# Latent attention queries made token-major by fours of heads and turned by TensorE, with changes of order in the gates and at the start

## The chip, the cores and the metric

The kernel is one program on one core of a Trainium2 chip. The metric is the device time of one execution in microseconds (us), as the median of repeated runs. Profiles are of one further execution of the same program.

## What is computed

Two transformer blocks are applied to one sequence of 256 tokens, 1024 channels wide, all in 32-bit floats. The part that the change rewrites is the second attention of the second block: its queries come from a latent of 768 channels, 96 channels a head, are normalised over these 96, and the last 32 of them are rotated by position.

```python
qb = jnp.einsum('bsr,re->bse', rms_norm_2(c_q, cq_norm_g), w_uq)
qb = qb.reshape(b, s, N_HEADS_B, QK_HEAD_DIM_B)          # 8 heads x (64 + 32)
...
qb = rms_norm_2(qb, qnorm_b_g)
kb = rms_norm_2(kb, knorm_b_g)
qb = jnp.concatenate([qb[..., :QK_NOPE_DIM],
                      apply_rope(qb[..., QK_NOPE_DIM:], positions)], axis=-1)
kb = jnp.concatenate([kb[..., :QK_NOPE_DIM],
                      apply_rope(kb[..., QK_NOPE_DIM:], positions)], axis=-1)
out_b = causal_block_attention(qb, kb, vb).reshape(b, s, WIDTH_B)
```

apply_rope multiplies the 32 channels by cosines and adds the same channels, their halves swapped, times signed sines. Before all this stands a first block (a gated linear recurrence, a spatial gate, three gate projections, a wide feed-forward layer), and in the second block another attention (heads of 64 channels) shares the stretch with the latent one.

## The kernel before

**Weights.** All weights stream through four slots of `raw` (128 x 2048 floats, a "unit"), brought by DMAs of the SP queue as soon as unit u-4 has been used (`unit_used`). ScalarE (ACT in the profile) rounds a unit to `whi` (`split_hi`, called three units ahead as `ahead(u)`), VectorE (DVE) makes the remainder `wlo` (`split_lo`), and TensorE (PE) computes each product in three matmuls (`mm3`: whi with xh, whi with xl, wlo with xh).

**Order.** Every engine runs one program that is written out by hand, and waits on semaphores. Nothing is reordered at run time, so an instruction that waits holds up everything behind it on its engine.

**The attention stretch.** There are eight pairs of heads, p = 0 to 3 of the first attention and 4 to 7 of the latent one. For each pair, `qk(p)` makes logits on PE, `logits_row(p)` scales and biases them on DVE, `softmax_exp(p)` is on ACT, `normalise(p)` on DVE, `turn(p)` transposes the probabilities on PE, `probs_copy(p)` copies them on ACT, `pv(p)` multiplies them with the values on PE, and `heads_hi(p)`, `heads_lo(p)` split the result. Between these steps PE is given other work: the latent queries (`queries`, six calls of eight blocks, while pairs 0 to 3 pass), the keys' transposes (`keys_turned`), and the output projection (`wo_part`). A head's queries are channel-major: the weights stand still in PE, 256 tokens stream, and the rows 96 to 127 of a head hold a second copy of its last 32 channels, halves swapped (the weights hold these columns twice).

**Queries on other engines.** `queries_evac(j)` (ACT, four calls, one for two heads) copies the swapped rows, squares, and copies with the gain, and signals `uq_ev`. GpSimd (POOL) runs `rotate(j)`, three operations of 32 x 512, and signals `q_rot`. `queries_stats(j)` (PE) sums the squares over channels with 16 tiny matmuls, DVE adds epsilon (`queries_factor`), and POOL's `head_factors` takes the power -1/2. PE's `qk(p)` of a latent pair waits for `q_rot`.

**Gates and start.** In units U_GA to U_GB+3 ACT first rounds the next unit and then evacuates the finished gate with its sigmoid or silu. At the start PE runs 14 products of ones before the first real product, and the input's four parts and the first weights arrive in the order of `PIECES`.

Of the kernel before, what the change touches and what calls it, by code (L numbers as in the profile page):

```python
# [68 lines left out]
HEADS_BANK = (7,) * 7 + (4,)  # L69

# [100 lines left out]
PIECES = ((0, 1), (2,), (3, 4), (5, 6, 7, 8, 9))  # L171
# [27 lines left out]

def raw_count(u):  # L200

    return 16 * sum(2 if by_rows(v) else 1 for v in range(u % SLOTS, u + 1, SLOTS))
# [35 lines left out]
def build_blocks(nc, w, xT, pT, par, cst, lvl, sgw, sgb, lnr, rel, oneh, maskb, pos, out):  # L238
    scratch = nc.dram_tensor("bias_scratch", [HEADS, 512], F32, kind="Internal").ap()
    ctx = ExitStack()  # L240
    with ctx:
# [31 lines left out]
        gkb = sb("gkb", [P, 1])  # L273
        nti = sb("nti", [P, 32], I32)
# [15 lines left out]
        def keys_part(v):  # L290

            return v[:, U_UK % SLOTS, :].rearrange("p (n c) -> p n c", c=P)[:, :, 0:64]

# [73 lines left out]
        qb, kb, qsw, sqq = view(48, 8), view(56, 8), view(64, 8), view(72, 8)  # L367
# [8 lines left out]
        cosk, sink, cosq, sinq = (view(80 + i, 1) for i in range(4))  # L376
# [11 lines left out]
        def _(sp):  # L388
# [7 lines left out]
            for u in range(3, UNITS):  # L396
                if u >= SLOTS:
                    sp.wait_ge(sem("unit_used"), u + 1 - SLOTS)
                if by_rows(u):
                    for i in range(2):  # L400
                        dst = raw[:, u % SLOTS, 1024 * i:1024 * i + 1024].rearrange("p (n c) -> p n c", n=2)
                        src = w[stored(u - u % 2 + i)].rearrange("p (n c) -> p n c", n=2)[:, :, columns(u % 2)]
                        sp.dma_start(dst, src).then_inc(sem(f"raw_in{u % SLOTS}"), 16)
                else:
                    sp.dma_start(raw[:, u % SLOTS, :], w[stored(u)]).then_inc(sem(f"raw_in{u % SLOTS}"), 16)
# [8 lines left out]
        def _(pool):  # L414
            pool.dma_start(cst_s[:, :], cst).then_inc(sem("cst_in"), 16)
            nc.gpsimd.memset(half_s[:, :], -0.5).then_inc(sem("half"), 1)
            pool.wait_ge(sem("half"), 1)
            pool.wait_ge(sem("raw_in3"), 16)
# [68 lines left out]
            pool.dma_start(ang[64:96, 0, :].bitcast(I32), pos[0:1, :].broadcast_to([32, T])).then_inc(sem("pos_in"), 16)  # L487
# [11 lines left out]
            def rotate(j):  # L499

                pool.wait_ge(sem("uq_ev"), j + 1)
                q_, w_ = qb[64:96, 2 * j:2 * j + 2, :], qsw[64:96, 2 * j:2 * j + 2, :]
                nc.gpsimd.tensor_tensor(q_, q_, cosq[64:96, 0:1, :].broadcast_to([32, 2, T]), ALU.mult).then_inc(sem("rot"), 1)
                nc.gpsimd.tensor_tensor(w_, w_, sinq[64:96, 0:1, :].broadcast_to([32, 2, T]), ALU.mult).then_inc(sem("rot"), 1)
                pool.wait_ge(sem("rot"), 2 * j + 2)
                nc.gpsimd.tensor_tensor(q_, q_, w_, ALU.add).then_inc(sem("q_rot"), 1)
                pool.wait_ge(sem("q_rot"), j + 1)

            head_factors("sk", 32, 16)
            pool.wait_ge(sem("rope"), 1)  # L510
            for j in range(4):
                rotate(j)
                head_factors("sq", 48 + 4 * j, 4, j + 1)
            for s in ("bias_in", "pos_in", "maskb_in"):
# [5 lines left out]
        def _(act):  # L520
            A = nc.scalar.activation

            def split_hi(u):
# [3 lines left out]
                hi, full = (keys_part(v) if u == U_UK else v[:, slot, :] for v in (whi, raw))  # L527
# [123 lines left out]
            for u in range(4, 32):  # L651
# [6 lines left out]
                if u == U_WB - 1:  # L658
                    heads_hi_turned(0)
                    heads_hi_turned(1)  # L660
                if not U_ZI <= u < U_GA:
# [27 lines left out]
                elif u % 2 == 1:  # L689
                    dst, func, m = ((ga, ACT.Sigmoid, u - U_GA) if u < U_ZG else  # L690
                                    (zg, ACT.Silu, u - U_ZG) if u < U_GB else (gb, ACT.Sigmoid, u - U_GB))
                    filled(u)
                    for s in range(2):
                        evac(u - 1 + s, dst[:, s, columns(m // 2)], func, scale=rtok[:, 0, s:s + 1])
# [216 lines left out]
            def rope_copy():  # L911
# [3 lines left out]
                for t in range(2):  # L915
                    A(krt_sq[:, t, :], src[:, t, 0:32], ACT.Square, accum_out=rs[:, 16 + t:17 + t])
                A(krt, src[:, :, 32:64], ACT.Copy).then_inc(sem("krt"), 1)
# [6 lines left out]
            def queries_evac(j):  # L924
                if j < 3:
                    act.wait_ge(sem("uq_mm"), j + 1)
                else:
                    filled(U_UQ + 2)
                b = j % 3
                src = ps[b][0:96, :].rearrange("p (h t) -> p h t", h=2)  # L930
                hs = slice(2 * j, 2 * j + 2)
                A(qsw[64:96, hs, :], ps[b][96:128, :].rearrange("p (h t) -> p h t", h=2), ACT.Copy)
                A(sqq[0:96, hs, :], src, ACT.Square)
                A(qb[0:96, hs, :], src, ACT.Copy, scale=col("qb", 0, 0, 96)).then_inc(sem("uq_ev"), 1)
# [14 lines left out]
            heads_hi(0)  # L949
            queries_evac(0)  # L950

# [4 lines left out]
            queries_evac(1)  # L956
            queries_evac(2)

            probs_copy(2)
            softmax_exp(3)  # L960
            heads_hi(2)
# [4 lines left out]
            queries_evac(3)  # L966

            for i in range(4, 6):
                probs_copy(i - 1)
                softmax_exp(i)  # L970
                heads_hi(i - 1)
                if i == 4:
                    keys_evac(2)
                    keys_evac(3)
                normalise_second(i)
# [53 lines left out]
        def _(dve):  # L1029
# [12 lines left out]
            def split_lo(u):  # L1042

                slot = u % SLOTS
                dve.wait_ge(sem("hi_ready"), u + 1)
                lo, full, hi = (keys_part(v) if u == U_UK else v[:, slot, :] for v in (wlo, raw, whi))
# [461 lines left out]
            def logits_row(p):  # L1508
# [3 lines left out]
                if p >= 4:  # L1512
                    dve.wait_ge(sem("sq_fac"), p - 3)
                for hh in range(2):
# [3 lines left out]
                    r0, r1 = (h, 16 + h) if p < 4 else (48 + 4 * (p - 4) + hh, 48 + 4 * (p - 4) + 2 + hh)  # L1518
# [1239 lines left out]
```

## Time and profile before

| what | value |
|---|---|
| median of 3 runs | 817.52 us (816.78 to 817.81) |
| the profiled execution | 817.01 us, of which the span from first to last instruction is 814.8 us |
| PE busy | 807.4 us, 99% of the span |
| DVE, ACT, POOL busy | 578.2, 466.0, 116.0 us (71%, 57%, 14%) |
| TensorE's granted clock | 1.000 of full speed |
| DMA | 143.85 MB, mean 177 GB/s |

Busy time of PE counts overlapping matmuls once, so 99% says that PE is hardly ever without a matmul, not that it is at its peak. The distance from the start of one group of matmuls to the start of the next is what a group costs.

### The profile page before, as it was taken

How to read it: one execution, taken by the hardware profiler on the slowest of the kernel's cores; microseconds unless marked ns; L12 is line 12 of the kernel's file. 1: busy time of each engine (PE TensorE's matmuls, PEld its weight loads, DVE VectorE, ACT ScalarE, POOL GpSimd, SP SyncE). 2: the span in 40 equal slices, each digit the busy share in tenths (PEclk: the TensorE clock that was granted, in tenths of full speed). 3: DMA queues.
4: the chain of work that ended last, by engine and by line, in shares of the span. 5: the costliest groups of instructions: out<-in, count | busy, mean ns of one | idle time of the engine just before them, and what ended most of it. 6: DMA issues, size and time to landing. Idle time of an engine off the chain costs nothing.

```text
span 814.8 us, 14269 instructions
## 1 busy us (share of the span) xinstructions
PE 807.4 (99%) x6160; PEld 715.4 (88%) x6160; DVE 578.2 (71%) x717; ACT 466.0 (57%) x602; POOL 116.0 (14%) x78
## 2 busy tenths in 40 slices
PE   9999999999999999999999999999999999999998
PEld 8999988788788998888888799998899888888886
DVE  6868995896666677666666687698967866556653
ACT  7679774563634674445544565456887644544442
POOL 0102780672000000000000000000482000000000
PEclk9999999999999999999999999999999999999999
DMA  9844444444553655555556555555332655555641
GB/s 316 294 157 162 159 169 133 156 158 155 168 205 108 234 181 187 180 201 197 172 200 202 171 198 186 182 173 191 105 104 74 218 180 202 197 173 198 207 156 51
DMA packets 30222, 143.85 MB, mean 177 GB/s; under 512 B 2978, under 2 KB 5042, under 8 KB 15824
## 3 DMA queue, kind: packets, MB, share of 16 engines
q1 hardware_dynamic: 28976, 139.47, 50.0%
q0 software_dynamic: 1040, 3.43, 1.2%
q8 instruction: 48, 0.79, 0.4%
q14 instruction: 14, 0.11, 0.0%
q10 hardware_dynamic: 144, 0.04, 0.0%
HBM read 141.87 MB, written 1.06 MB: 175 GB/s over the span
## 4 chain that ended last, share of the span: by engine, by line
PE 95%; DVE 2%; ACT 1%; DMA 1%; issue 1%; POOL 0%; SPq 0%
PE ps L1829 8%; PE ps L1830 8%; PE ps L1831 8%; PE ps L2235 7%; PE ps L2228 7%; PE ps L2140 6%; PE ps L2142 6%; PE ps L2141 6%; PE ps L1897 5%; PE ps L1900 4%; PE ps L1903 4%; PE ps L2233 4%; PE ps L2230 4%; PE ps L2006 1%; DMA raw<-w 1%; PE ps L1855 1%
## 5 line engine op out<-in xcount | busy, mean ns | idle before, releaser
L1047 DVE TENSOR_TENSOR wlo<-raw,whi 128x2048 fp32r<-128x2048 f32 x128 | 292.8, 2289 | 85.9 <-ACT whi L528 84.6
L528 ACT ACTIVATE whi<-raw 128x2048 fp32r<-128x2048 f32 x128 | 243.8, 1906 | 140.4 <-DMA raw<-w 140.4
L1829 PE MATMUL ps<-xx,whi 128*128 128x256 f32 x552 | 159.2, 288 | 0.0
L1830 PE MATMUL ps<-xx,whi 128*128 128x256 f32 x552 | 156.1, 283 | 0.0
L1831 PE MATMUL ps<-xx,wlo 128*128 128x256 f32 x552 | 156.1, 283 | 0.0
L1829 PEld LDWEIGHTS ps<-xx,whi 128*128 128x128 f32 x552 | 105.7, 191 | 1.5 <-issue 0.7
L1830 PEld LDWEIGHTS ps<-xx,whi 128*128 128x128 f32 x552 | 105.8, 192 | 0.1
L1831 PEld LDWEIGHTS ps<-xx,wlo 128*128 128x128 f32 x552 | 105.7, 192 | 0.0
L2140 PE MATMUL ps<-whi,xx 128*128 128x512 f32 x216 | 84.1, 390 | 0.0
L2141 PE MATMUL ps<-whi,xx 128*128 128x512 f32 x216 | 84.1, 389 | 0.0
L2142 PE MATMUL ps<-wlo,xx 128*128 128x512 f32 x216 | 84.0, 389 | 0.0
L1897 PE MATMUL ps<-whi,xx 128*128 128x512 f32 x176 | 70.5, 401 | 0.7 <-ACT work L540 0.7
L1399 DVE TENSOR_TENSOR work<-ps,work 128x256 f32<-128x256 f32 x64 | 26.8, 420 | 62.6 <-ACT work L763 62.6
L447 POOL TENSOR_TENSOR work<-work 128x512 f32<-128x512 f32 x28 | 58.7, 2117 | 84.3 <-DVE work L1191 45.3
L1900 PE MATMUL ps<-whi,xx 128*128 128x512 f32 x176 | 68.7, 390 | 0.0
L1903 PE MATMUL ps<-wlo,xx 128*128 128x512 f32 x176 | 68.6, 390 | 0.0
L2235 PE MATMUL ps<-xx,whi 128*128 128x512 f32 x256 | 64.1, 392 | 0.0
L2228 PE MATMUL ps<-xx,whi 128*128 128x512 f32 x256 | 63.3, 389 | 0.0
L2228 PEld LDWEIGHTS ps<-xx,whi 128*128 128x128 f32 x256 | 47.9, 188 | 10.0
L2235 PEld LDWEIGHTS ps<-xx,whi 128*128 128x128 f32 x256 | 46.0, 189 | 8.2
L767 ACT ACTIVATE xx<-work 128x512 fp32r<-128x512 f32 x27 | 17.1, 633 | 57.3 <-DVE work L1421 26.9
L2142 PEld LDWEIGHTS ps<-wlo,xx 128*128 128x128 f32 x216 | 40.5, 188 | 8.4
(298 smaller groups left out, 1272.7 us busy)
## 6 DMA issues: line engine op xcount, KB each, us to landing
raw<-w SPq DMA_DIRECT2D x112, 1024.0 KB, 4.9
raw<-w SPq DMA_DIRECT2D x34, 512.0 KB, 5.0
raw<-w SPq DMA_DIRECT2D x8, 256.0 KB, 6.6
x<-xT SPq DMA_DIRECT2D x4, 256.0 KB, 5.5
work<-bias_scratch POOLq DMA_DIRECT2D x1, 1024.0 KB, 8.2
out<-x SPq DMA_DIRECT2D x3, 256.0 KB, 2.5
work<-lnr POOLq DMA_DIRECT2D x1, 512.0 KB, 6.5
work<-sgw POOLq DMA_DIRECT2D x1, 512.0 KB, 7.2
```

The source lines that it names most:

```text
L528: A(hi, full, ACT.Copy).then_inc(sem("hi_ready"), 1)
L1047: V.tensor_tensor(lo, full, hi.bitcast(F32), ALU.subtract)\
L1829: mm(out, hi, xh[:, tile, :], start=start, stop=False, skip_group_check=skip)
L1830: mm(out, hi, xl[:, tile, :], start=False, stop=False, skip_group_check=skip)
L1831: return mm(out, wlo[:, slot, at:at + width], xh[:, tile, :], start=False, stop=stop, skip_group_check=skip)
L1897: mm(o, xh[:, t, xs], wh, start=first, stop=False)
L1900: mm(o, xl[:, t, xs], wh, start=False, stop=False)
L2140: mm(o, xh[:, base + kk, xs], whi[:, slot, wc], start=first, stop=False, skip_group_check=True)
L2141: mm(o, xl[:, base + kk, xs], whi[:, slot, wc], start=False, stop=False, skip_group_check=True)
L2142: return mm(o, xh[:, base + kk, xs], wlo[:, slot, wc], start=False, stop=end, skip_group_check=True)
L2228: mm(o[:, :], whi[:, u % SLOTS, w(k)], xx[:, base + k, :, :], start=k == 0, stop=False)
L2235: last = mm(o[:, :], whi[:, u % SLOTS, w(k)], xx[:, base + k, :, :], start=False, stop=k == 7, skip_group_check=True)
```

## The change

The queries of four heads are now made token-major: 128 tokens stand still in PE and 384 columns of weights (four heads of 96) stream, so that tokens lie on partitions. The doubled weight columns are not loaded: units U_UQ, U_UQ+1 and U_UQ+2 are gathered by 5, 9 and 4 DMAs with rows of 96 columns, and hold 5, 5 and 2 steps of 384 columns. `queries_evac(g)` (two calls) takes two PSUM banks each with a square and a copy of 128 x 384; DVE sums the squares along the free axis; POOL rotates on 128 partitions, four operations for four heads and 128 tokens; PE then transposes the result (`queries_turned(j)`, four transposes, four calls) and ACT copies it with the gain (also named `queries_turned(j)`, signal `q_n`). The cosine and sine table is transposed too, and copied by ACT (`qrope`) before `krt` is signalled.

```diff
 (PE)
-            for n in range(14):
+            for n in range(11):
...
-            def queries_stats(j):
-                pe.wait_ge(sem("uq_ev"), j + 1)
-                pe.wait_ge(sem("head_ml"), j + 2)
-                for s in range(2):
-                    for hh in range(2):
-                        last = head_stats(272 + 4 * j + 2 * s + hh, sqq, 2 * j + hh, s)
...
+                    for t in range(2):
+                        if k == 0 and (g, t) != (0, 0):
+                            if (g, t) == (1, 1):
+                                pe.wait_ge(sem("uq_ev"), 1)
+                            else:
+                                pe.wait_ge(sem("uk_ev"), g + 1)
+                        o = ps[QUERY_BANKS[g][t]][:, 0:384]
+                        xs, wc = slice(t * P, (t + 1) * P), slice(384 * at, 384 * at + 384)
+                        mm(o, xh[:, k, xs], whi[:, u % SLOTS, wc], start=k == 0, stop=False)
+                        mm(o, xl[:, k, xs], whi[:, u % SLOTS, wc], start=False, stop=False)
+                        last = mm(o, xh[:, k, xs], wlo[:, u % SLOTS, wc], start=False, stop=k == 5)
...
+            def queries_turned(j):
+
+                pe.wait_ge(sem("q_rot"), 2 * (j // 2) + 2)
+                if j % 2:
+                    pe.wait_ge(sem("q_n"), j)
+                for hh in range(2):
+                    for t in range(2):
+                        last = nc.tensor.transpose(ps[TURN_BANKS[j]][0:96, hh * T + t * P:hh * T + (t + 1) * P],
+                                                   qtok[:, t, 2 * j + hh, :], ident)
+                last.then_inc(sem("qt_mm"), 1)
...
-            queries(32, 40)
+            queries(4)
+            queries_turned(0)
             qk(3)
             turn(2)
-            queries_stats(0)
-            queries(40, 48)
+            queries(5)
+            queries_turned(1)
             pv(2)
             keys_turned(0)
+            pe.wait_ge(sem("q_n"), 2)
             pe.wait_ge(sem("uq_ev"), 3)
             wo_part(0, 0, range(4), (1, 2))
...
 (POOL)
-            pool.dma_start(cst_s[:, :], cst).then_inc(sem("cst_in"), 16)
...
+            pool.wait_ge(sem("x_in3"), 16)
+            pool.dma_start(cst_s[:, :], cst).then_inc(sem("cst_in"), 16)
 (ACT)
+                if u in (U_GA, U_ZG, U_GB):
+                    A(warm[:, :], half_s[:, 0:1], ACT.Silu if u == U_ZG else ACT.Sigmoid)
+                if u >= U_GA and u % 2 == 1:
+                    dst, func, m = ((ga, ACT.Sigmoid, u - U_GA) if u < U_ZG else
...
+                    filled(u)
+                    for s in range(2):
+                        evac(u - 1 + s, dst[:, s, columns(m // 2)], func, scale=rtok[:, 0, s:s + 1])
                 if not U_ZI <= u < U_GA:
                     ahead(u)
 (DVE)
-                factor_input("sq", ps[7][:, a:a + 4], 48 + 4 * j, 4, 96)
+                link(V.reduce_sum(sums, qsq[g].rearrange("p s (h c) -> p (s h) c", c=96), AX))
+                V.tensor_scalar(sums, sums, 96 * EPS, None, ALU.add).then_inc(sem("sq_eps"), 1)
```

PE around the fifth pair, in the kernel before: the tail of `turn(3)` (L2410), then the 16 small sums of `queries_stats(1)` (L1923), the output products (L1829 to L1831, twelve in all, three shown), `pv(3)` (L2431 to L2435), `keys_turned(1)` (L2463) and the next output product.

```order
L2410 MATMUL ps<-cst_s,work 128x128 x5
L1923 MATMUL ps<-cst_s,work 32x1 [waits head_ml,uq_ev]
L1923 MATMUL ps<-cst_s,work 32x1 x15
L1829 MATMUL ps<-xx,whi 128x256 [waits head_ml]
L1830 MATMUL ps<-xx,whi 128x256
L1831 MATMUL ps<-xx,wlo 128x256
...
L2435 MATMUL ps<-work 64x128 x2
L2463 MATMUL ps<-cst_s,work 96x128 [waits head_l,k_n]
L2463 MATMUL ps<-cst_s,work 96x128 x7
L1829 MATMUL ps<-xx,whi 128x256 [waits head_ml,lo_ready,uq_ev]
```

The same place in the changed kernel (the lines' numbers have moved):

```order
L2478 MATMUL ps<-cst_s,work 128x128 x5
L2572 MATMUL ps<-cst_s,work 96x128 [waits q_rot]
L2572 MATMUL ps<-cst_s,work 96x128 x3
L1897 MATMUL ps<-xx,whi 128x256 [waits head_ml]
L1898 MATMUL ps<-xx,whi 128x256
L1899 MATMUL ps<-xx,wlo 128x256
...
L2500 MATMUL ps<-work 64x128 x2
L2572 MATMUL ps<-cst_s,work 96x128 [waits q_n,q_rot]
L2572 MATMUL ps<-cst_s,work 96x128 x3
L2518 MATMUL ps<-cst_s,work 96x128 [waits head_l,k_n]
L2518 MATMUL ps<-cst_s,work 96x128 x7
L1897 MATMUL ps<-xx,whi 128x256 [waits head_ml,lo_ready,q_n]
```

The 16 sums are gone, two groups of four transposes (L2572) have come in, and the second group and the output product behind the keys' transposes now wait for `q_n`, a copy on ACT.

ACT at the fifth pair in the changed kernel: `softmax_exp(4)` (L939), `queries_turned(2)` (L999), `heads_hi(3)` (L958), `keys_evac(2)` and `keys_evac(3)` (L983), `queries_turned(3)` (L999), `normalise_second(4)` (L947).

```order
L939 ACTIVATE work<-work 128x128 [waits head_l]
L939 ACTIVATE work<-work 128x256
L939 ACTIVATE work<-work 128x128
L939 ACTIVATE work<-work 128x256
L999 ACTIVATE work<-ps0,gqb 96x512 [waits qt_mm]
L958 ACTIVATE xx<-ps7 128x256 [waits head_pv]
L983 ACTIVATE work<-ps4,gkb 96x512 [waits kt_mm]
L983 ACTIVATE work<-ps3,gkb 96x512 [waits kt_mm]
L999 ACTIVATE work<-ps0,gqb 96x512 [waits qt_mm]
L947 ACTIVATE work<-work 128x128 [waits head_rec]
```

In the kernel before the two rows L999 are not there, and the same ten places hold only the exponentials, `heads_hi(3)`, the two `keys_evac` and `normalise_second(4)`.

POOL, the power for the keys (L547 of the changed kernel) and the rotation of the first four heads, as it is now:

```order
L547 TENSOR_TENSOR nt<-nt,half_s 128x16 [waits sk_eps]
L556 TENSOR_TENSOR work<-work 128x128 [waits uq_ev,krt,sk_fac]
L560 TENSOR_TENSOR work<-work 128x4x16 x2
L562 TENSOR_TENSOR work<-work 128x4x32 [waits rot]
L556 TENSOR_TENSOR work<-work 128x128 [waits uq_ev,q_rot]
L560 TENSOR_TENSOR work<-work 128x4x16 x2
L562 TENSOR_TENSOR work<-work 128x4x32 [waits rot]
L547 TENSOR_TENSOR nt<-nt,half_s 128x8 [waits sq_eps,q_rot]
```

Before, three operations of 32x512 stood here for two heads, and PE's first reader of them was `qk(4)`; now eight smaller ones stand for four heads, and PE's first reader is `queries_turned(0)`, ahead of `qk(3)`.

## Rows read from the trace of the kernel before

**Rows 1.** The page, first part: busy time, share, instructions.

```profile
PE 807.4 (99%) x6160; PEld 715.4 (88%) x6160; DVE 578.2 (71%) x717; ACT 466.0 (57%) x602; POOL 116.0 (14%) x78
```

**Rows 2.** Waits of PE: total us, times, longest us.

```profile
PE ps L1897 <- ACT work L540: 0.7, 1, 0.7
```

**Rows 3.** Timeline of PE: start, us, first block of queries, second pair.

```profile
565.16 0.38 PE L1829 MATMUL ps<-xx,whi 128*128 128x256 f32 x1
...
568.22 0.49 PE L2397 MATMUL ps<-work 64*128 64x128 f32 x4
...
569.08 0.88 PE L2410 MATMUL ps<-cst_s,work 128*128 128x128 f32 x6
```

**Rows 4.** Timeline of PE, from the fourth pair to the fifth.

```profile
585.03 0.49 PE L2397 MATMUL ps<-work 64*128 64x128 f32 x4
...
586.93 0.43 PE L1923 MATMUL ps<-cst_s,work 96*32 96x1 f32 x32
...
591.16 1.08 PE L2463 MATMUL ps<-cst_s,work 128*96 128x128 f32 x8
592.00 0.36 PE L1829 MATMUL ps<-xx,whi 128*128 128x256 f32 x1
...
594.95 0.61 PE L2397 MATMUL ps<-work 96*128 96x128 f32 x4
...
600.63 0.36 PE L1829 MATMUL ps<-xx,whi 128*128 128x256 f32 x1
```

**Rows 5.** Timeline of ACT: krt's copy, a pair's copies, exponentials, keys' copies.

```profile
568.63 0.24 ACT L917 ACTIVATE work<-ps 128x64 f32<-128x64 f32 x1
...
578.40 0.87 ACT L893 ACTIVATE work<-ps 128x384 f32<-128x384 f32 x2 [1.92 <-PE ps L2410]
...
588.79 0.40 ACT L879 ACTIVATE work<-work 128x128 f32<-128x128 f32 x1 [0.17 <-DVE work L1531]
...
590.47 0.19 ACT L879 ACTIVATION_READ_ACCUMULATOR work<-work 128x1 f32 x1
...
591.84 1.26 ACT L922 ACTIVATE work<-ps,gkb 96x512 f32<-96x512 f32 x2 [0.18 <-PE ps L2463]
```

**Rows 6.** Timeline of DVE: keys' scaling; end of the fifth pair's logits.

```profile
580.06 1.23 DVE L1689 TENSOR_TENSOR work<-work,nt 128x1024 f32<-128x1024 f32 x1
581.20 2.92 DVE L1692 TENSOR_TENSOR work<-work,nt 128x256 f32<-128x256 f32 x2
...
597.92 0.08 DVE L1523 DVE_READ_ACCUMULATOR2_ANT work<- 128x1 f32 x1
```

**Rows 7.** Timeline of POOL: powers (L495) and rotations (L503).

```profile
577.11 2.92 POOL L495 TENSOR_TENSOR nt<-nt,half_s 128x16 f32<-128x16 f32 x1 [54.02 <-DVE nt L1680]
580.11 2.30 POOL L503 TENSOR_TENSOR work<-work 32x512 f32<-32x512 f32 x1
...
605.43 1.01 POOL L495 TENSOR_TENSOR nt<-nt,half_s 128x4 f32<-128x4 f32 x1 [0.21 <-DVE nt L1504]
606.52 1.27 POOL L503 TENSOR_TENSOR work<-work 32x512 f32<-32x512 f32 x1
```

**Rows 8.** Timeline of PE, opening.

```profile
1.04 6.24 PE L1982 MATMUL ps<-work 128*128 128x128 f32 x28 [1.04 <-DVE work L1100]
7.04 0.71 PE L1950 MATMUL ps<-whi,xx 128*128 128x512 f32 x2
...
18.40 0.28 PE L1971 MATMUL ps<-xx,whi 128*128 128x256 f32 x1
```

**Rows 9.** Timeline of ACT, opening: the first weights' rounding.

```profile
5.91 0.63 ACT L569 ACTIVATE whi<-raw 128x512 fp32r<-128x512 f32 x1 [0.18 <-DMA raw<-w]
```

**Rows 10.** DMA issues: KB each, us to landing.

```profile
cst_s<-cst POOLq DMA_DIRECT2D x1, 99.0 KB, 5.1
```

**Rows 11.** Timeline of ACT at the gates.

```profile
206.33 1.28 ACT L540 ACT_TABLE_LOAD   x1
207.63 1.27 ACT L540 ACTIVATE work<-ps,rtok 128x512 f32<-128x512 f32 x2
```

More of the change, by code:

```diff
@@ L197, in by_rows, with query_place, query_runs, transfers @@
     return U_GA <= u < U_WB or U_WA <= u < U_WOUT
+QUERY_STEPS = (((0, 0), (0, 1), (0, 2), (0, 3), (0, 4)),
+               ((0, 5), (1, 0), (1, 1), (1, 2), (1, 3)),
+               ((1, 4), (1, 5)))
+def query_place(g, k):
+    n = next(n for n in range(3) if (g, k) in QUERY_STEPS[n])
+    return n, QUERY_STEPS[n].index((g, k))
+def query_runs(n):
+    runs = []
+    for h in range(HEADS):
+        ks = [k for g, k in QUERY_STEPS[n] if g == h // 4]
+        for u in range(3):
+            here = [k for k in ks if (6 * h + k) // 16 == u]
+            if here:
+                runs.append((h, here[0], len(here), u, (6 * h + here[0]) % 16))
+    return runs
+def transfers(u):
+    if U_UQ <= u < U_WO:
+        return len(query_runs(u - U_UQ))
+    return 2 if by_rows(u) else 1
 def raw_count(u):
-    return 16 * sum(2 if by_rows(v) else 1 for v in range(u % SLOTS, u + 1, SLOTS))
+    return 16 * sum(transfers(v) for v in range(u % SLOTS, u + 1, SLOTS))
 def z_index(u):
@@ L497, in head_factors, with rotate @@
                 pool.wait_ge(sem(name + "_fac"), turn)
[L499 to L507, printed above, removed]
[L509 to L514 removed]
+            def rotate(g, t):
+                n = 2 * g + t + 1
+                pool.wait_ge(sem("uq_ev"), n)
+                q_ = qtok[:, t, 4 * g:4 * g + 4, 64:96]
+                nc.gpsimd.tensor_tensor(turn_a, q_, qrope[:, t:t + 1, 0:32].broadcast_to([P, 4, 32]), ALU.mult).then_inc(sem("rot"), 1)
+                for half in range(2):
+                    other = qtok[:, t, 4 * g:4 * g + 4, 80 - 16 * half:96 - 16 * half]
+                    sines = qrope[:, t:t + 1, 32 + 16 * half:48 + 16 * half].broadcast_to([P, 4, 16])
+                    nc.gpsimd.tensor_tensor(turn_b[:, :, 16 * half:16 * half + 16], other, sines, ALU.mult).then_inc(sem("rot"), 1)
+                pool.wait_ge(sem("rot"), 3 * n)
+                nc.gpsimd.tensor_tensor(q_, turn_a, turn_b, ALU.add).then_inc(sem("q_rot"), 1)
+                pool.wait_ge(sem("q_rot"), n)
+            head_factors("sk", 32, 16)
+            pool.wait_ge(sem("krt"), 1)
+            for g in range(2):
+                rotate(g, 0)
+                rotate(g, 1)
+                head_factors("sq", 48 + 8 * g, 8, g + 1)
+            pool.wait_ge(sem("p_in"), 32)
+            for s in ("bias_in", "maskb_in"):
                 pool.wait_ge(sem(s), 16)
@@ L2481, in _, with queries @@
             rope_turned()
-            def queries(first, end):
-                for i in range(first, end):
-                    n, blk = divmod(i, 16)
-                    h, k = divmod(i, 6)
-                    j, u = h // 2, U_UQ + n
-                    if blk == 0:
+            def queries(i):
+                g, part = divmod(i, 3)
+                for k in (2 * part, 2 * part + 1):
+                    n, at = query_place(g, k)
+                    u = U_UQ + n
+                    if at == 0:
```

123 lines of the change are left out of this document (65 added, 58 removed).

## The prediction

> **What bounds the kernel now.** I read the page first, then the waits of PE, then the timelines of PE, ACT, DVE and POOL through the attention stretch, and last the opening and the gates. The page shows PE busy for 99% of the span [rows 1], and apart from the start its longest wait is 0.7 us, for a gate's evacuation [rows 2]. So time is what PE is given to do: a change gains what it takes off PE and loses every new wait of PE. Whether a wait is new is read from chains on ACT, DVE and POOL, whose shares look harmless as averages.
>
> **What PE is given less.** One block of query products, 24 matmuls of 256 columns, runs from 565.16 to the second pair's `qk` at 568.22, 3.06 us, or about 0.12 a matmul with 0.17 for entering [rows 3]. The new block has 12 matmuls of 384 columns. None of that width is in the trace. The 48 opening products of 512 columns take at most 11.36 us, 0.237 each [rows 8]; half-way between 0.12 and 0.237 is 0.178, and 12 of these with the entry are 2.3 us. Six blocks give -0.76 each, -4.6. The bounds are those of a matmul, 0.12 and 0.237: -8.7 to -0.3; half-way is near, since width is all that differs. The four groups of small sums take 0.43 each [rows 4]: -1.7. Sixteen transposes come in; eight of the keys' take 0.84 (591.16 to 592.00), 0.105 each [rows 4]: +1.7, and two for the position table +0.2. Net -4.4 us. If nothing waited, this would be the gain of the stretch.
>
> **What PE then waits for.** I walk it in the times of the trace, four places in order.
>
> First turn. PE would come to `turn(0)` at 565.16 + 0.2 + 2.3 + 0.86 (the step from 568.22 to 569.08 [rows 3]) = 568.5. It waits for `krt`, which ACT signals after the copy at 568.63 [rows 5], and the copy of the table now goes ahead of it with 0.2 to 0.25. So 569.1: PE waits 0.6, and is where it was before.
>
> First turning of queries. PE comes there after four more blocks, four times 0.76 earlier than before, at about 582.0. It waits for both rotations of the first four heads, which stand on POOL behind the power for the keys, 2.92 us for 16 elements [rows 7]. That power started at 577.11. It comes about 1.7 earlier: `qk(1)` is 0.56 earlier, and DVE's remainder of the last query unit shrinks by 1280 columns, 1.5 us at 1.23 per 1024 [rows 6], less 0.4 in which DVE then waits for ACT's exponentials. So it ends at 578.3. A rotation is four POOL operations, on 128, 64, 64 and 128 elements. 512 elements take 1.27 when nothing disturbs [rows 7]. Scaled by elements that gives 0.32 and 0.16; with the fixed part of the powers (16 elements 2.92, 4 elements 1.01, so 0.16 an element and 0.37 fixed) it gives 0.6 and 0.5. I take 0.45 and 0.3: two rotations 3.2 us with signals (2.0 to 4.5).
>
> POOL does not have this time to itself. The rotation at 580.11 took 2.30 against 1.27 of the same operation at 606.52 [rows 7], and it ended 1.1 us after DVE's scaling of the keys at 580.06 (1.23) had; the two following scalings of 256 elements took 2.92 together where 1.23 per 1024 gives 0.7 [rows 6]. These two engines take turns. Beside the new rotations stand the same three scalings (1.9) and the third pair's four normalisations (about 1.0), 2.9 in all; I take 2.3, since some fall where POOL waits for its own signals. Rotations end at 578.3 + 3.2 + 2.3 = 583.8. PE waits 1.8 us (0 if nothing is held, 3.7 by the upper bounds). The Trainium skill, in SBUF — State Buffer, section Who interferes with whom, says that a DVE instruction with two inputs in SBUF and a GpSimd instruction that reads it exclude each other for their whole length. By that rule all 2.9 are held and PE waits 2.4; the rows 6 and 7 agree with it, 2.30 against 1.27. With 0.45 for the transposes `qk(3)` is at 584.25 instead of 585.03: 0.8 early.
>
> Output products behind the keys' transposes. They use banks that ACT must have emptied of turned queries (`q_n` 2). From `qk(3)` to them it was 592.00 - 585.03 = 6.97 [rows 4]. Now the chain is: `qk` and DVE's logits to the start of the exponentials 3.4 (it was 588.79 - 585.03 = 3.76, with DVE late from its own work [rows 4, 5]), exponentials 1.8 (588.79 to 590.66 [rows 5]), four reads of 128 x 384 at 0.87 a pair, 1.6 [rows 5], a copy of 96 x 512, 0.6 (two take 1.26 [rows 5]), a signal 0.1: 7.5. So 0.5 is lost here, and 0.3 is left of the lead.
>
> Fifth pair. From `qk(4)` to the next output product it was 600.63 - 594.95 = 5.68 [rows 4], full of work. Now there are two hand-overs in a row. Logits end at 598.00, 3.05 after `qk(4)` [rows 4, 6], exponentials 1.8, the copy 0.6, signals 0.1: the fourth turning can start 5.55 after `qk(4)`. Then on PE its four transposes and four of the keys', 0.85, a latency of 0.25, on ACT two keys' copies 1.2 and the last queries' copy 0.6: 2.95 with signals. Together 8.5, 2.8 more than before. Behind the waiting matmul on PE stands the whole rest of the stretch, and its lead is gone: 2.5 late. The third and fourth groups of sums, 0.9, fall away after this place: +1.6 us at the end of the stretch. Sums and waits agree: -4.4 from work, +0.6, +1.8, and some 3.6 in the last two places.
>
> **The other parts.** Gates: the evacuation at 207.63 stood behind the rounding of the next unit and a table load of 1.28 [rows 11]; the gate's product is done before, and the load is now made early by a dummy. The 0.7 wait goes [rows 2]: -0.7 (0 to -0.8). Opening: three of 14 products of ones go, 6.0 / 14 each, so PE is free at 5.8 instead of 7.04 [rows 8], and its first weights are rounded at 5.91 + 0.63 = 6.5 [rows 9]: up to -0.5 there; of the 11.36 up to 18.40 [rows 8] some 0.4 are waits for parts in an order that now suits it better. Against this the constants leave 12 us later, took 5.1 us to land [rows 10], and PE wants them right after these products. I take -0.6 (0 to -1.0). The gathers of 96 columns have no row; ACT's idle time hides them, and late ones would delay the first exponentials.
>
> **Sum.** +1.6 - 0.7 - 0.6 = +0.3 on the profiled execution's 817.0, which is 0.5 below the median of the runs shown; against the median, 817.5 + 0.3 = 817.8 us. About 1.6 us either way, 0.2%, is what a measurement of this kernel can tell from no change.
>
> **Rivals.** (a) Rotations are short and not held, and ACT's copies fit beside other steps: the 1.8 go, and about half of the 2.8; the stretch ends at -1.5, the kernel at 814.8. For it: POOL is busy 14%. Against: the 2.30 against 1.27 of rows 7. (b) No new wait lasts: -4.4 - 0.7 - 0.6 = -5.7, 811.8 us. For it: 99% busy PE and all its work counted. Against: a chain from `qk(4)` that row by row is 8.5 us long. (c) Slower: POOL is the bound. With 0.6 and 0.5 an operation and 2.9 held, the first turning waits 3.7 instead of 1.8, and the second group, which starts only after its own power, comes late for the third turning by about 0.8; +0.3 + 2.7 = 820.5 us. It decides from about 0.55 an operation. (d) Slower: PE, idle for 2 us at a time where 0.7 was the longest, loses clock. The trace before grants full clock throughout. One block (2.3) and one pair's steps (1.5) at half speed would cost 3.8: 821.6 us. The skill's TensorE: Matmul & The Clock Gate, section What's actually happening, has the clock fall behind idle PE; no row here shows it.
>
> **How the numbers follow.** Forecast 0.40 (its own range 816.2 to 819.4), (a) 0.24, (b) 0.10, (c) 0.23, (d) 0.03. The range reaches past (a) and (c) and leaves out (b) and (d) and a little more: 813.6 to 820.8. Faster by over 0.2%: (a), (b) and 0.02 of the forecast, 0.36. Slower: (c), (d) and 0.04, 0.30. Within: 0.34.
>
> **What would show it.** Right: PE's waits list four new ones, for ACT's `krt` copy (0.6), for POOL's sum (about 1.8), and twice for ACT's copy of turned queries (about 1.5 each), and the gate's 0.7 is gone; DVE idles before the fourth pair's logits; a block of products takes 2.2 to 2.4. Wrong: POOL's operations well under 0.3 or over 0.55 us; a granted clock below 1; PE waiting for `cst_in` or for a gathered unit; and any chain of ACT that runs shorter than its rows say.

## The result and the profile after

The changed kernel takes 821.19 us (median of 10 runs, 819.7 to 825.12), the kernel before on the same chip 817.58 us (10 runs). The ratio is 1.004, with a 95% interval of 1.0024 to 1.0057: slower by 2.0 to 4.7 us. The forecast was 817.8 us with no measurable change, and the range ended at 820.8; both missed.

The profiled execution took 821.01 us with a span of 819.2, where that of before had 814.8. The page of the changed kernel, busy time, beside [rows 1]:

```profile
PE 803.3 (98%) x5972; PEld 708.3 (86%) x5972; DVE 574.4 (70%) x719; ACT 463.3 (57%) x606; POOL 102.1 (12%) x80
```

PE is busy for 4.1 us less, and the span is 4.4 us longer. So the work did come off, and 8.5 us of idle PE came in. The view of PE's waits says where, beside [rows 2] (total us, times, longest us):

```profile
PE ps L1897 <- ACT work L999: 2.9, 2, 1.5
PE ps L2039 <- DMA cst_s<-cst: 1.8, 1, 1.8
PE ps L2572 <- POOL work L562: 1.4, 1, 1.4
PE ps L2557 <- ACT work L969: 1.4, 1, 1.4
PE ps L2050 <- DVE work L1167: 1.0, 1, 1.0
PE ps L2572 <- ACT work L999: 0.9, 1, 0.9
PE ps L2018 <- ACT whi L627: 0.8, 1, 0.8
...
PE ps L2133 <- DVE work L1287: 0.4, 1, 0.4
...
PE ps L2296 <- DVE work L1460: 0.3, 1, 0.3
```

Three of these the prediction had announced: the products behind `q_n` (2.9 in two places), the turning of queries behind GpSimd (1.4, forecast 1.8) and the turning behind ACT (0.9). Two its sum had not: 1.8 for the constants, which it only lists as a sign of being wrong, and 1.4 for L969, which is the keys' copy. A fourth that it had announced, 0.6 for `krt`, is not there. The 0.8 for the first rounded weights (L627) is the idle time that it expected when three products of ones go. The gate's wait of 0.7 is gone.

The timeline of PE in the changed kernel gives the ledger; the first row is the opening, the second is beside [rows 3], the others beside [rows 4]:

```profile
20.07 0.39 PE L2039 MATMUL ps<-xx,whi 128*128 128x256 f32 x1 [1.75 <-DMA cst_s<-cst]
...
567.18 0.44 PE L2557 MATMUL ps<-whi,xx 128*128 128x384 f32 x1
...
569.38 0.44 PE L2557 MATMUL ps<-whi,xx 128*128 128x384 f32 x1 [1.41 <-ACT work L969]
...
586.40 0.64 PE L2572 MATMUL ps<-cst_s,work 128*96 128x128 f32 x4 [1.42 <-POOL work L562]
586.97 0.49 PE L2465 MATMUL ps<-work 64*128 64x128 f32 x4
...
594.41 0.39 PE L1897 MATMUL ps<-xx,whi 128*128 128x256 f32 x1 [1.37 <-ACT work L999]
...
597.37 0.61 PE L2465 MATMUL ps<-work 96*128 96x128 f32 x4
...
603.05 0.61 PE L2572 MATMUL ps<-cst_s,work 128*96 128x128 f32 x4 [0.87 <-ACT work L999]
...
606.02 0.39 PE L1897 MATMUL ps<-xx,whi 128*128 128x256 f32 x1 [1.48 <-ACT work L999]
...
647.49 0.39 PE L2208 MATMUL ps<-whi,xx 128*128 128x512 f32 x1
```

The last row is the second feed-forward's first product of the 128x512 form; before it was

```profile
643.16 0.39 PE L2140 MATMUL ps<-whi,xx 128*128 128x512 f32 x1
```

From the first query product to that product is what I call the stretch: 643.16 - 565.16 = 78.00 us before, 647.49 - 567.18 = 80.31 after, +2.3. The opening is later by 20.07 - 18.40 = 1.7 [rows 8]. Between these two, from 20 to 567 us, another 0.35 is lost, although the gate's wait of 0.7 is gone: 0.4 of the 1.05 that came in is a wait at the transposes near 218 us (L2133) and 0.3 one near 313 us (L2296).

| part | forecast | measured in the two profiles |
|---|---|---|
| opening | -0.6 | +1.7 |
| 20 to 567 us, the gates in it | -0.7 | +0.35 |
| attention stretch | +1.6 | +2.3 |
| sum | +0.3 | +4.4 |

### The profile page after: what moved, and what is told of

The parts are those of the page before. It is cut to its first block, busy times and chain, and to the rows that moved or that the text cites. A ratio compares the mean times of both kernels' runs of the same rounds, so it can differ in the third digit from the quotient of the medians.

```text
span 819.2 us, 13913 instructions
## 1 busy us (share of the span) xinstructions
PE 803.3 (98%) x5972; PEld 708.3 (86%) x5972; DVE 574.4 (70%) x719; ACT 463.3 (57%) x606; POOL 102.1 (12%) x80
## 4 chain that ended last, share of the span: by engine, by line
PE 56%; DVE 2%; ACT 2%; POOL 1%; issue 0%; DVEq 0%; POOLq 0%
PE ps L2303 7%; PE ps L2296 7%; PE ps L2210 6%; PE ps L2209 6%; PE ps L2208 6%; PE ps L2301 4%; PE ps L2298 4%; PE ps L1897 4%; PE ps L1898 3%; PE ps L1899 3%; ACT work L939 1%; PE ps L1923 1%; PE ps L1928 1%; PE ps L1924 1%; PE ps L2467 1%; DVE work L1588 1%
## 5 line engine op out<-in xcount | busy, mean ns | idle before, releaser
L1114 DVE TENSOR_TENSOR wlo<-raw,whi 128x2048 fp32r<-128x2048 f32 (+1 forms) x128 | 291.0, 2275 | 87.1 <-ACT whi L586 85.7
L586 ACT ACTIVATE whi<-raw 128x2048 fp32r<-128x2048 f32 (+1 forms) x128 | 242.5, 1896 | 121.1 <-DMA raw<-w 120.9
L1897 PE MATMUL ps<-xx,whi 128*128 128x256 f32 x504 | 145.0, 288 | 2.9 <-ACT work L999 2.9
L1898 PE MATMUL ps<-xx,whi 128*128 128x256 f32 x504 | 142.6, 283 | 0.0
L1899 PE MATMUL ps<-xx,wlo 128*128 128x256 f32 x504 | 142.5, 283 | 0.0
L1897 PEld LDWEIGHTS ps<-xx,whi 128*128 128x128 f32 x504 | 96.5, 192 | 4.4 <-ACT work L999 3.4
L1898 PEld LDWEIGHTS ps<-xx,whi 128*128 128x128 f32 x504 | 96.6, 192 | 0.1
L1899 PEld LDWEIGHTS ps<-xx,wlo 128*128 128x128 f32 x504 | 96.6, 192 | 0.0
L2296 PE MATMUL ps<-xx,whi 128*128 128x512 f32 x256 | 63.4, 389 | 0.3 <-DVE work L1460 0.3
L2296 PEld LDWEIGHTS ps<-xx,whi 128*128 128x128 f32 x256 | 47.9, 188 | 10.6 <-issue 0.7
L2303 PEld LDWEIGHTS ps<-xx,whi 128*128 128x128 f32 x256 | 46.0, 189 | 8.2
L823 ACT ACTIVATE work<-ps 128x256 f32<-128x256 f32 x64 | 23.9, 373 | 43.3 <-PE ps L2298 39.0
```

The lines of the kernel that those rows point to most:

```text
L586: A(hi, full, ACT.Copy).then_inc(sem("hi_ready"), 1)
L1114: V.tensor_tensor(lo, full, hi.bitcast(F32), ALU.subtract)\
L1897: mm(out, hi, xh[:, tile, :], start=start, stop=False, skip_group_check=skip)
L1898: mm(out, hi, xl[:, tile, :], start=False, stop=False, skip_group_check=skip)
L1899: return mm(out, wlo[:, slot, at:at + width], xh[:, tile, :], start=False, stop=stop, skip_group_check=skip)
L2296: mm(o[:, :], whi[:, u % SLOTS, w(k)], xx[:, base + k, :, :], start=k == 0, stop=False)
```

## The experiments

The first four kernels cut the change into its parts. The stretch turned out to be a fine ruler: in the profiles of the three of them whose queries are those of before it is 78.00, 78.04 and 78.02 us, so a tenth of a microsecond in it means something, which in the whole time it does not. With the new queries in the changed kernel's order it is 80.31, and 80.34, 80.35 and 80.32 us in e4, e5 and e11.

**e1, the opening alone, on the kernel before.**

```diff
-PIECES = ((0, 1), (2,), (3, 4), (5, 6, 7, 8, 9))
+PIECES = ((0, 1), (2, 3), (4, 5), (6, 7, 8, 9))
-            pool.dma_start(cst_s[:, :], cst).then_inc(sem("cst_in"), 16)
+            pool.wait_ge(sem("x_in3"), 16)
+            pool.dma_start(cst_s[:, :], cst).then_inc(sem("cst_in"), 16)
-            for n in range(14):
+            for n in range(11):
```

> The kernel before with the opening's edits alone (pieces, 11 warming products, constants issued behind the fourth part of x). Late constants: the first product starts about 0.7 us earlier, the first products end about 18.2, then PE waits about 1.7 us for the DMA of the constants, the next product starts near 20.1 instead of 18.4, and the kernel is 1.5 to 1.8 us slower (about 819.3), all of it ahead of 21 us. Rival, that the wait belongs to something else of the change (the longer programs, other traffic): the next product starts at 17.8 to 18.4 and the time is 817.0 to 817.8.

820.07 us against 817.87, ratio 1.003 (1.0013 to 1.0046): the opening costs 1.1 to 3.8 us by itself. Its profile, PE's timeline:

```profile
19.49 0.44 PE L1972 MATMUL ps<-xx,whi 128*128 128x256 f32 x1 [1.93 <-DMA cst_s<-cst]
19.73 0.41 PE L1973 MATMUL ps<-xx,whi 128*128 128x256 f32 x1
```

The wait is there, 1.93. But behind it these products follow each other by 0.21 us, where before they did by 0.12. The stretches of the same profile (start and end, length, PE busy, granted clock, DMA share, GB/s) say why:

```profile
18.00:20.00 2.00, 0.51 (x3) 0.92 1.02 427
20.00:22.00 2.00, 2.00 (x11) 0.50 0.96 393
22.00:24.00 2.00, 2.00 (x27) 0.73 0.98 385
```

The granted clock fell to 0.50, the 1.2 GHz level, after PE had stood idle for 1.9 us, and came back at about 23 us; 1.6 us more are lost in that: from the product at 19.49 to the same later mark it is 5.86 us (25.35), before 4.25 (18.40 to 22.65). In the profile of the changed kernel the same wait, 1.75, left the clock at 1.00. So the late constants cost a wait of 1.8 to 2.2 us in every profile that has them this late (1.75, 1.93, and 2.20, 2.14, 2.17 in e6, e7 and e10), and in some executions nearly as much again. The record has the mean granted clock of every execution of e1: six with 0.999 or 1.000 took 818.7 us in the median, six with 0.995 to 0.998 took 821.0. That the first six are only 0.8 above the kernel before fits the profile, where the first products end 1.0 us earlier (17.56 against 18.56).

**e2, the gates' order alone, on the kernel before**: the dummy activations and both evacuations ahead of the next unit's conversion.

```diff
+                if u in (U_GA, U_ZG, U_GB):
+                    A(warm[:, :], half_s[:, 0:1], ACT.Silu if u == U_ZG else ACT.Sigmoid)
+                if u >= U_GA and u % 2 == 1:
...
+                    filled(u)
+                    for s in range(2):
+                        evac(u - 1 + s, dst[:, s, columns(m // 2)], func, scale=rtok[:, 0, s:s + 1])
                 if not U_ZI <= u < U_GA:
                     ahead(u)
...
-                elif u % 2 == 1:
```

> The kernel before with the gates' order alone (table load ahead, both evacuations ahead of the next unit's conversion). Theory of giving back: the wait of 0.72 at the first gate unit goes, but the conversion of the next unit on ACT starts about 2 us later, so DVE splits later, and waits of about 0.3 to 0.4 come at the forward transposes near 218 and at the products near 312: net between -0.3 and +0.5 us (817.3 to 818.1). Rival, my prediction's own step: the wait goes and nothing comes back, -0.7 (816.9).

816.82 us, ratio 0.9986 (0.9976 to 0.9997), -0.2 to -2.0 us. The gate's wait is gone and the wait near 218 did not come; my theory of giving back falls. A wait of 0.8 near 380 us came (below).

**e3, only the dummy activations.**

```diff
+                if u in (U_GA, U_ZG, U_GB):
+                    A(warm[:, :], half_s[:, 0:1], ACT.Silu if u == U_ZG else ACT.Sigmoid)
```

> The kernel before with only the one-element activations that load the table ahead of the first gate unit, evacuations left behind the conversion. The 1.28 us of table load leave the stretch between conversion and evacuation, so the evacuation starts near 206.3 instead of 207.6 and PE's wait of 0.72 there goes; the conversions keep their place, so no wait comes back: -0.7 us (816.9). Rival: the load ahead of the conversion delays the conversion by its own 1.28, and the waits near 218 and 312 come as in the run with the full order: about 0.

817.32 us, ratio 0.9992 (0.9981 to 1.0003). In its trace ACT's evacuation starts at 206.61, right behind the conversion, and PE does not wait. The time agrees with -0.7 and with 0; that the wait goes is shown, its value is not.

**e4, the queries alone**, with the opening and the gates' order as before.

> The changed kernel with the opening and the gates' order put back, so that only the queries' part of the change is left. If the parts are additive it is the attention's own +2.3 us of the profile: stretch from the first query product to the first unit of the second feed-forward 2.3 longer, time 819.9. Rival, that the attention stretch only pays because everything before it came 2 us late (DMA times do not shift with it): the stretch is less than 1 us longer and the time within 0.8 of before.

821.7 us, ratio 1.0041 (1.0026 to 1.0056). The stretch is 80.34 us, +2.3 as in the whole change, with the same five waits to a tenth. It starts elsewhere in time, so where transfers happen to stand has no part in it. The rival falls. The rest of its loss lies ahead of the queries: 1.6 for ACT near 145 us (0.4 before) and 1.0 for DVE near 380 us. Such waits are in nearly every profile here, with other sizes each time (near 145: 0.5, 1.0, 0.7 in e1 to e3; near 380: 0.8 and 0.5 in e2 and e3), with and without any of the edits. I take them as what one execution differs by from the next, and the 1.05 between 20 and 567 us in the changed kernel's profile with them: e5 and e6 have the same gates and neither the wait near 218 nor that near 313. The three parts add up within their intervals: +2.4 (e1), -1.1 (e2) and +3.4 (e4) are +4.7, where the whole change has 2.0 to 4.7.

The next four start from the changed kernel.

**e5, the constants issued first again.**

```diff
+            pool.dma_start(cst_s[:, :], cst).then_inc(sem("cst_in"), 16)
...
-            pool.wait_ge(sem("x_in3"), 16)
-            pool.dma_start(cst_s[:, :], cst).then_inc(sem("cst_in"), 16)
```

> The changed kernel with the constants issued first again, the new pieces and 11 warming products kept. Late constants: the wait of 1.8 for them goes, and with it any stretch at half clock behind it; the constants now share the queues with the first pieces, so 0 to 1 us of waits for pieces may come: 1 to 2.5 us faster than the changed kernel (818.7 to 820.2). Rival, that taking the constants from the head was worth what was forecast for it (0.6): the first products end 0.6 later than in the changed kernel and the time is the same within 1 us.

820.21 us against 818.28, ratio 1.0029 (1.0016 to 1.0041). The wait is gone from the list, and the same product starts at 18.50 instead of 20.07. By the ratios that is about 0.9 us, and the two intervals overlap, so the time does not tell the expectation from its rival; by the trace it is 1.6. The first products end at 18.66 here, at 18.31 in the changed kernel and at 18.56 before.

**e6, the keys' first copy ahead of the first exponentials on ACT.**

```diff
-            softmax_exp(0)
             keys_copy(0)
+            softmax_exp(0)
```

> The changed kernel with the copy of the keys' first tile ahead of the first exponentials on ACT. Theory, a bank that the copy frees late: PE's wait of 1.4 at the second bank of the first block goes, the keys' logits and the first turn come 1.4 earlier, 819.8. Rival: the exponentials and with them the first turn come later by what the copy takes, so that the same wait stands at the first turn instead: 0 to -0.5 us (820.7 to 821.2).

820.07 us, ratio 1.0016 (1.0001 to 1.0031). The stretch is 78.84, 1.5 shorter than in the changed kernel. The wait of 1.4 is gone; 0.4 for L978 (`krt`) stands at the first turn instead, and the wait for GpSimd is 1.1 instead of 1.4. That 0.4 is the wait of 0.6 of my prediction: in the changed kernel it was hidden behind the one that I had missed.

**e7, another order for the same work**: one step on PE, four on ACT.

```diff
             queries(4)
-            queries_turned(0)
             qk(3)
             turn(2)
+            queries_turned(0)
...
-            queries_turned(0)
-
             probs_copy(2)
-            softmax_exp(3)
+            queries_turned(0)
             queries_evac(1)
             queries_turned(1)
+            softmax_exp(3)
...
                 probs_copy(i - 1)
-                softmax_exp(i)
                 if i == 4:
                     queries_turned(2)
+                softmax_exp(i)
...
+                    queries_turned(3)
                     keys_evac(2)
                     keys_evac(3)
-                    queries_turned(3)
```

> The changed kernel with another order for the same work: on PE the first turned pair of queries behind the third turn of probabilities; on ACT both copies of the second pair and the evacuations of the second four heads ahead of the exponentials of row 3, the third pair's copy ahead of the exponentials of row 4, the fourth's ahead of the keys' last two. Theory that the stretch loses its time to the places of these steps (1.4 for GpSimd, 1.4, 0.9 and 1.5 for ACT): -3.5 to -5.1 (816.1 to 817.7). Rival, that ACT has too much work there (1.9 of conversion, 1.8 of exponentials and 3.6 of copies in each turn), so that the waits only move to the turns and the keys: 0 to -1.5 (819.7 to 821.2).

817.13 us, ratio 0.9995 (0.9981 to 1.0009). The stretch is 75.63, 4.7 shorter than in the changed kernel. In place of the four waits of 1.4, 1.4, 0.9 and 1.5 there are two, of 0.4 for DVE and 0.3 for ACT. ACT had room for everything; it had it in the wrong order.

**e8, everything together**: e6 and e7, the table load of e3 in place of the gates' order, and the constants issued behind the second part of x (`x_in1`).

> The changed kernel with the early copy, the new order of both engines, the constants issued behind the second part of x, the gates' evacuations back behind the conversions and only the table load ahead. If the causes are these three and add up: 1.4 + 4 + 1.8 off, 813 to 815, faster than the kernel before by 0.3 to 0.6%. Rival, that the queries' form itself is the dearer one: not below 817.6.

813.45 us, ratio 0.9942 (0.9924 to 0.996): faster than the kernel before by 3.3 to 6.2 us. By the ratios that is 8.0 us less than the changed kernel, where the causes were expected to add up to 7.2.

**e9, e4 with the edits of e6 and e7**: nothing of the opening and the gates.

> The queries' part of the change alone (opening and gates' order as before), with the early copy of the keys and the new order of PE and ACT. If the new form is cheaper once its waits are gone (work -4.4 by the prediction's sum, remaining new waits about 0.7), the stretch from the first query product to the first unit of the second feed-forward is 3.0 to 4.0 us shorter than before (66.5 there) and the time 814 to 815. Rival, that the gain of the run with everything came from the opening and the gates: the stretch is within 1 us of before, and the time 817 to 818.

813.73 us against 817.65, ratio 0.9953 (0.9937 to 0.9968). PE's timeline:

```profile
565.90 0.44 PE L2553 MATMUL ps<-whi,xx 128*128 128x384 f32 x1
...
589.05 0.36 PE L1893 MATMUL ps<-xx,whi 128*128 128x256 f32 x1 [0.41 <-DVE wlo L1110]
...
598.54 0.36 PE L1893 MATMUL ps<-xx,whi 128*128 128x256 f32 x1 [0.30 <-ACT work L996]
...
639.97 0.39 PE L2204 MATMUL ps<-whi,xx 128*128 128x512 f32 x1
```

The stretch is 639.97 - 565.90 = 74.07, 3.9 shorter than before, with 0.7 of new waits in it. (The 66.5 that the expectation gives for the stretch before is not the length between these two products; that is 78.00.) The query form by itself is the gain, and nearly all of e8's.

**e10, both rotations of the first heads ahead of the keys' reciprocal roots on GpSimd**, the rest as in the changed kernel.

```diff
-            head_factors("sk", 32, 16)
             pool.wait_ge(sem("krt"), 1)
...
+            rotate(0, 0)
+            rotate(0, 1)
+            head_factors("sk", 32, 16)
```

> The changed kernel with both rotations of the first four heads ahead of the keys' reciprocal roots on GpSimd. The wait of 1.4 at the first turned pair goes; but the keys' roots end about 3.5 us later, VectorE's product with them stands ahead of its normalisation of row 2, and so the third turn of probabilities waits 1 to 2.5 us instead: 820.5 to 822.5. Rival, that the order on GpSimd alone holds the pair and VectorE has room: -1.4 (819.8).

823.33 us, ratio 1.0072 (1.0045 to 1.0099). The wait only moves: 2.2 for DVE at the third turn. GpSimd's timeline in it, first rotation,

```profile
580.49 0.45 POOL L556 TENSOR_TENSOR work<-work 128x128 f32<-128x128 f32 x1 [55.82 <-ACT work L996]
580.91 0.59 POOL L560 TENSOR_TENSOR work<-work 128x64 f32<-128x64 f32 x2
581.58 0.46 POOL L562 TENSOR_TENSOR work<-work 128x128 f32<-128x128 f32 x1
```

and that of the changed kernel, where DVE scales the keys from 581.64 to 583.94:

```profile
578.70 2.91 POOL L547 TENSOR_TENSOR nt<-nt,half_s 128x16 f32<-128x16 f32 x1 [53.84 <-DVE nt L1749]
581.69 1.50 POOL L556 TENSOR_TENSOR work<-work 128x128 f32<-128x128 f32 x1
583.16 0.96 POOL L560 TENSOR_TENSOR work<-work 128x64 f32<-128x64 f32 x2
584.21 0.47 POOL L562 TENSOR_TENSOR work<-work 128x128 f32<-128x128 f32 x1
```

In e10 DVE does logits and reductions beside it, and nothing is held. The first two rotations take 3.2 us there (580.49 to 583.67) and 4.65 in the changed kernel (581.69 to 586.34), 1.5 more, of which 1.4 is in the first three rows. DVE was held too. Its scalings of the keys (L1758, L1761) and its normalisation (L1606, L1607) in the changed kernel:

```profile
581.64 1.23 DVE L1758 TENSOR_TENSOR work<-work,nt 128x1024 f32<-128x1024 f32 x1 [0.20 <-POOL nt L547]
582.78 1.16 DVE L1761 TENSOR_TENSOR work<-work,nt 128x256 f32<-128x256 f32 x2
...
584.27 0.56 DVE L1607 TENSOR_SCALAR work<-work 128x256 f32<-128x256 f32 x1
584.75 0.55 DVE L1606 TENSOR_SCALAR work<-work 128x128 f32<-128x128 f32 x1
585.21 0.42 DVE L1607 TENSOR_SCALAR work<-work 128x256 f32<-128x256 f32 x1
```

and in e10, where GpSimd does nothing beside them:

```profile
587.84 0.75 DVE L1763 TENSOR_TENSOR work<-work,nt 128x256 f32<-128x256 f32 x2
...
588.92 0.35 DVE L1609 TENSOR_SCALAR work<-work 128x256 f32<-128x256 f32 x1
589.18 0.28 DVE L1608 TENSOR_SCALAR work<-work 128x128 f32<-128x128 f32 x1
589.38 0.35 DVE L1609 TENSOR_SCALAR work<-work 128x256 f32<-128x256 f32 x1
```

So DVE lost 0.4 in the scalings and 0.55 in the normalisation. And the clock fell here too, which I had not expected; stretches of e10:

```profile
568.00:570.00 2.00, 0.82 (x4) 0.93 0.74 311
570.00:572.00 2.00, 2.00 (x9) 0.50 0.43 180
572.00:574.00 2.00, 2.00 (x15) 0.71 0.00 0
...
588.00:590.00 2.00, 0.22 (x2) 1.00 0.92 389
590.00:592.00 2.00, 2.00 (x10) 0.55 0.27 107
```

The first fall stands behind the wait of 1.41 for the keys' copy, the same wait as in the changed kernel, whose profile shows 1.00 there. It cost 1.5 us more, and the second fall, behind the wait of 2.2, 1.6. That is why the time lies above the range of the expectation; all four executions of e10 have a mean clock of 0.996 to 0.998. Its wait of 2.2 for the constants, earlier in the same execution, left the clock at 1.00.

**e11, the constants later still**, behind the third unit (`raw_in3` for `x_in3`).

> The changed kernel with the constants issued later still, behind the last part of the third unit (near 20 us instead of 14.3), to price the late transfer: it lands near 26, PE waits about 7.5 instead of 1.8, and if the clock falls behind such a wait, as in the profile of the run with the opening alone (granted 0.50 from 20 to 22 us), the products behind it cost 1.5 to 2 more: 827 to 829. Rival, that waiting costs only its own time and much of it is taken up again by transfers that then stand ready: 824 to 826, clock 1.00 behind the wait.

829.34 us, ratio 1.014 (1.011 to 1.017). The wait is 7.7, the product starts at 25.73, and the granted clock is 0.50 from 20 to 30 us. The products behind the wait lost 1.9 more against the changed kernel by 30 us. The rival, waiting costs only itself, falls. The clock fell once more in this profile, behind a wait of 2.1 for DVE, which cost 1.7 more. Its wait, and the stretches behind it:

```profile
PE ps L2296 <- DVE work L1460: 2.1, 1, 2.1
...
322.00:324.00 2.00, 1.51 (x6) 0.94 0.88 369
324.00:326.00 2.00, 2.00 (x8) 0.50 0.28 119
```

**e12, e8 with the whole opening as before.**

> The run with everything, with the whole opening as before (pieces, 14 warming products, constants first). If the new pieces with constants in time are worth what was forecast (0.6): 814.0, first products ending 0.5 later. Rival, that without the late constants the opening is worth nothing either way: within 0.5 of the run with everything (813.0 to 813.9).

813.61 us, ratio 0.9941 (0.992 to 0.9962), where e8 has 0.9942. The difference is far inside the two intervals, each some 3 us wide, so the time tells neither the forecast's 0.6 nor nothing. The traces say a little more. With the new pieces and 11 products of ones the first products end at 17.56 to 18.66 us in eight profiles, 18.30 in the mean; with the old opening at 18.18 to 19.46 in six, 18.74 in the mean. They suggest a gain of some 0.4, and single executions differ by more than that.

## Why the prediction was wrong, step by step

**Work taken off PE: right.** A block of the 384-column form takes 2.28 us (572.63 to 574.91), forecast 2.3. The stretch of the changed kernel is 2.3 longer with 6.55 of the new waits in it, so 4.2 of work left; e9 gives 3.9 + 0.7 = 4.6. Forecast was 4.4.

**The opening: the step that failed.** "Against this the constants leave 12 us later, took 5.1 us to land, and PE wants them right after these products. I take -0.6 (0 to -1.0)." The sentence holds all that was needed and never adds it up. GpSimd issued them at 14.26, they landed 5.8 later at 20.07, and PE's products ended near 18.3: +1.7, outside its bounds and with the wrong sign. GpSimd's issue before, in the changed kernel, and its landing there:

```profile
1.25 0.76 POOL L415 DMA_DIRECT2D cst_s<-cst  x1 [0.82 <-POOLq L2752]
...
14.26 0.76 POOL L469 DMA_DIRECT2D cst_s<-cst  x1 [13.43 <-DMA x<-xT]
...
cst_s<-cst POOLq DMA_DIRECT2D x1, 99.0 KB, 5.8
```
From the trace of before alone, the issue at 1.25 with 12 more and 5.1 to land is 18.4, against products that the term itself lets end at 17.8: 0.6 of wait, which eats the whole 0.6. The landing then came 1.7 later than that, because the fourth part of x landed 1.0 later than the 12 allow and the constants themselves took 0.7 longer. The gain itself, 0.6 for pieces and products of ones, is neither shown nor refuted (e12). And the wait sometimes takes the clock along (e1). The term measured +1.7 in the changed kernel's profile, 2.3 off, which is the largest part of the miss of 4.1, and 1.1 to 3.8 in e1.

**The first block: a wait that was not on the list.** I walked the first turn and found 0.6 for `krt`. But the new block writes two banks by turns, the second is the one that ACT's keys' copy empties, and the copy stands behind the exponentials of the first pair. The wait for it was in the diff, `uk_ev` ahead of the second bank's first product; I did not ask when ACT signals it. PE waits 1.4 there, and finds `krt` done at the turn: 0.8 more than forecast (e6 takes it away). So `qk(3)` came 0.1 earlier relative to the first query product (586.97 - 567.18 = 19.79 against 19.87), not 0.8.

**GpSimd: right in its rows, near in its sum partly by luck.** Two rotations take 3.2 when nothing holds them, as forecast; held 1.5 instead of 2.3; wait 1.4 instead of 1.8. Three sizes were off and in part cancel. Counted from the first query product, the keys' power ended at 14.4 (578.70 + 2.91 - 567.18) where 13.1 was forecast, GpSimd was held 0.8 less, and PE came at 17.8 (586.40 - 1.42 - 567.18) where 16.8 was forecast. The Trainium skill, in SBUF — State Buffer, section Who interferes with whom, has the engine that issues second wait for the other's whole instruction, whichever of the two it is. The prediction made of this that GpSimd would be held for all 2.9 of DVE's work. The traces agree with the page and not with that reading: the first operation of the rotations lost 1.05 (1.50 against 0.45) to a scaling of 1.23, GpSimd lost 1.5 in all, and DVE lost 0.4 in its scalings and 0.55 in its normalisation. e10 shows what the forecast did not name: another order on GpSimd only made another step wait; the pair's place on PE decides (e7).

**Products behind the keys' transposes: right.** From `qk(3)` to the first of them it is 594.41 - 586.97 = 7.44, forecast 7.5, before 6.97. To `qk(4)` it is 10.40 instead of 9.92, 0.5 lost, forecast 0.5. **Fifth pair: right.** From `qk(4)` to the output product 606.02 - 597.37 = 8.65, forecast 8.5, before 5.68. **Sums after it:** -1.1, forecast -0.9. The stretch so sums to -0.1 + 0.5 + 3.0 - 1.1 = +2.3 against +1.6, and the difference of 0.7 is that of the keys' copy.

**The gates: right in place.** The wait of 0.7 went, and e2 measures -0.2 to -2.0. In the changed kernel's profile other waits between 20 and 567 us took 1.05 back; what made them there and not in e5 and e6 stays open.

**The rivals.** (a), rotations that nothing holds, did not hold: they were held 1.5. (c), slower by a late GpSimd, was at 820.5, near the time that came, for a cause that did not hold: an operation took 0.45, under its point of 0.55. (d), the clock, had 0.03 and 821.6 us, the nearest number of all, and is not the cause either. It happens in some executions (e1, e10, e11) and not in the profiled one of the changed kernel. Of the ten timed executions of that kernel seven have a mean granted clock of 0.999 or 1.000, and their median is 821.01; the other three took 821.16, 821.37 and 825.12. So the median does not come from the clock, and the one time of 825 may. (b), all waits gone, at 811.8, is near what the form can give: e8 stands at 813.45.

## What to carry to other kernels

Where a transfer is moved behind something, write its landing as a time and set it beside the time at which it is wanted, before any value is chosen; a risk that is named but not added is no part of a sum. Where products are put into another order of banks, look for the last reader of every bank, on every engine, and put a time beside every semaphore wait that the diff adds: the keys' copy stood in it as `uk_ev`, and cost 1.4 us. And when less work comes back as waits of one engine's queue, the form need not be given up: six steps in another place (e6, e7) turned +2.3 us into -3.9 here.

## What the hardware did that I had not expected

- The granted clock fell to 0.50 (1.2 GHz) behind waits of PE of only 1.93 (e1), 1.41 and 2.2 (e10) and 2.1 us (e11), and stayed at 1.00 behind waits of 1.75 and 1.41 in the changed kernel, of 2.1 in e7 and of 2.2 in e6 and e10. Each fall cost 1.5 to 1.7 us on top of the wait. The Trainium skill's TensorE: Matmul & The Clock Gate, What's actually happening, has the clock fall behind idle PE, and these traces agree. But the same wait of 1.41 did it in one execution (e10) and not in another (the changed kernel).
- DVE's scalings in SBUF held GpSimd for 1.4 us, and GpSimd held DVE for 0.95 in the scalings and the normalisation behind them; DVE's logits, which read PSUM, and its reductions did not hold it at all (e10).
